# The second rows in front of a feed-forward: both engines evict every turned tile, in pairs

## The reference

```
x = layer_norm(ALPHA * x + 0.5 * swiglu(x, ffn1_w13[i], ffn1_w2[i]), ln_g[i, 0], ln_b[i, 0])
y = mixer(x) ; x = layer_norm(ALPHA * x + y, ln_g[i, 1], ln_b[i, 1])
x = layer_norm(ALPHA * x + 0.5 * swiglu(x, ffn2_w13[i], ffn2_w2[i]), ln_g[i, 2], ln_b[i, 2])

def swiglu(x, w13, w2):
    gate, up = jnp.split(x @ w13, 2, axis=-1)
    return (jax.nn.silu(gate) * up) @ w2
```

## Time and profile before

| | us |
|---|---|
| time, median of 3 runs | 2527.92 (2527.87 to 2528.9) |
| the profiled execution, its own time | 2527.56 |
| its span | 2525.8 |
| TensorE busy | 2463.6 (98%) |
| VectorE busy | 1505.4 (60%) |
| ScalarE busy | 1184.3 (47%) |
| GpSimd busy | 399.0 (16%) |

### The profile page before, as it was taken

The page is one execution under the profiler, slowest core; times in us unless marked ns, Lnnn a source line. Parts: engine busy times, 40 slices in busy tenths (PEclk is TensorE's granted clock), DMA queues, the critical chain, the costliest instruction groups (busy, mean ns, idle before and its releaser), DMA issues.

```text
span 2525.8 us, 32691 instructions
## 1 busy us (share of the span) xinstructions
PE 2463.6 (98%) x13213; PEld 2073.0 (82%) x13213; DVE 1505.4 (60%) x2146; ACT 1184.3 (47%) x1488; POOL 399.0 (16%) x463
## 2 busy tenths in 40 slices
PE   8999999999999999999989999999999999899999
PEld 6888878888888788888877888888878877898998
DVE  5546664464455645645566446446766567897644
ACT  5544554444444544444465444444554446444442
POOL 0002310000001100000131000001239802570000
PEclk9999999999999999999999999999999999999999
DMA  8554445555654455555334555555435543336553
GB/s 245 183 185 154 145 139 184 186 180 184 187 164 134 134 184 191 176 184 190 118 123 148 185 187 178 185 186 161 141 126 192 186 148 101 117 118 200 172 193 127
DMA packets 315542, 418.09 MB, mean 166 GB/s; under 512 B 18825, under 2 KB 273154, under 8 KB 315394
## 3 DMA queue, kind: packets, MB, share of 16 engines
q1 hardware_dynamic: 315394, 416.01, 51.2%
HBM read 414.92 MB, written 1.05 MB: 165 GB/s over the span
## 4 chain that ended last, share of the span: by engine, by line
PE 86%; DVE 6%; ACT 3%; issue 3%; POOL 1%; DMA 1%; SPq 0%; DVEq 0%; POOLq 0%; ACTq 0%
PE ps L597 25%; PE ps L599 24%; PE ps L598 24%; DVE wlo L469 2%; PE ps L614 2%; PE ps L2007 2%; PE ps L615 2%; PE ps L619 2%; PE ps L2264 1%; ACT whi L461 1%; PE ps L2313 1%; PE ps L2298 1%; PE ps L2253 1%; PE ps L1966 1%; DMA raw<-in_ffn_w_dram 1%
## 5 line engine op out<-in xcount | busy, mean ns | idle before, releaser
L469 DVE TENSOR_TENSOR wlo<-raw,whi 128x2048 fp32r<-128x2048 f32 (+1 forms) x397 | 909.5, 2296 | 608.3 <-ACT whi L461 607.5
L461 ACT ACTIVATE whi<-raw 128x2048 fp32r<-128x2048 f32 (+4 forms) x401 | 746.6, 1867 | 467.0 <-DMA raw<-in_ffn_w_dram 405.6
L597 PE MATMUL ps<-whi,xh 128*128 128x512 f32 (+3 forms) x1853 | 695.0, 375 | 8.5 <-DVE wlo L1386 2.5
L599 PE MATMUL ps<-whi,xl 128*128 128x512 f32 (+3 forms) x1853 | 687.7, 371 | 0.0
L598 PE MATMUL ps<-wlo,xh 128*128 128x512 f32 (+3 forms) x1853 | 687.3, 371 | 0.0
L597 PEld LDWEIGHTS ps<-whi,xh 128*128 128x128 f32 x1853 | 350.9, 189 | 73.7 <-issue 8.5
L599 PEld LDWEIGHTS ps<-whi,xl 128*128 128x128 f32 x1853 | 350.5, 189 | 60.0
L598 PEld LDWEIGHTS ps<-wlo,xh 128*128 128x128 f32 x1853 | 350.8, 189 | 57.8
L597 PE MATMUL ps<-whi,oh 128*128 128x512 f32 x944 | 380.0, 403 | 0.0
L599 PE MATMUL ps<-whi,ol 128*128 128x512 f32 x944 | 369.1, 391 | 0.0
L598 PE MATMUL ps<-wlo,oh 128*128 128x512 f32 x944 | 367.9, 390 | 0.0
(11 more groups left out here) (339 smaller groups left out, 2658.7 us busy)
## 6 DMA issues: line engine op xcount, KB each, us to landing
raw<-in_ffn_w_dram SPq DMA_DIRECT2D x352, 512.0 KB, 4.8
raw<-in_ffn_w_dram SPq DMA_DIRECT2D x88, 1024.0 KB, 4.9
raw<-in_w_ff_dram SPq DMA_DIRECT2D x32, 1024.0 KB, 5.3
raw<-in_w_out_dram SPq DMA_DIRECT2D x20, 1024.0 KB, 4.9
raw<-in_w_in_dram SPq DMA_DIRECT2D x20, 1024.0 KB, 5.1
raw<-in_dsa_w_in_dram SPq DMA_DIRECT2D x32, 512.0 KB, 4.8
raw<-in_dsa_w_in_dram SPq DMA_DIRECT2D x12, 1024.0 KB, 5.1
raw<-in_fox_w_in_dram SPq DMA_DIRECT2D x16, 512.0 KB, 4.6
```

The source lines that it names most:

```text
L461: act.activation(hi(u)[:, 0:w], raw[:, (slot[u] + 1) % SLOTS, 0:w], ACT.Copy).then_inc(sem("hi_ready"), 1)
L469: dve.tensor_tensor(lo(u)[:, 0:w], raw[:, (slot[u] + 1) % SLOTS, 0:w], hi(u)[:, 0:w].bitcast(F32), ALU.subtract).then_inc(sem("lo_ready"), 1)
L597: pe.matmul(o, ah, bh, start=start, stop=False, skip_group_check=True)
L599: return pe.matmul(o, al, bh, start=False, stop=stop, skip_group_check=True)
```

## The change

It concerns the second rows (t = 1) of the norms whose next stage is a feed-forward of the first block (`by_pairs`): seven of them. There `xT` is written by VectorE alone, all eight tiles, and `xh` by ScalarE alone, straight from PSUM with gain and shift in eight narrow activations instead of wide ones from `xT`. The turned tiles lie in banks 2, 3, 6 and 7 instead of 2, 5, 6 and 7. In each half ScalarE starts with the first two tiles and VectorE with the other two; then they change banks. The new semaphores `xh_half` and `xt_half` say that the first pair of each is done. VectorE takes the low part of a half directly behind that half's evictions. TensorE waits for both halves of `xn` before it turns the first one, begins the second rows' products with `xh_half`, and waits for the whole half (`middle`) in front of the third tile. GpSimd's `cx` waits for VectorE only.

```
+        if st["kind"] == "norm" and st["next"]["kind"] == "ffn":
+            made.update(xt_act=2, xh_half=2, xt_half=2)
...
-            first = 2 if t and st["next"]["kind"] == "ffn" else 4
-            bank = (first, 5, 6, 7)[k // 2]
+            bank = ((2, 3, 6, 7) if t and st["next"]["kind"] == "ffn" else (4, 5, 6, 7))[k // 2]
...
+        def by_pairs(st, t):
+            return t and st["kind"] == "norm" and st["next"]["kind"] == "ffn"
...
# token_major
                 for i, k in enumerate(ks):
+                    if i == 2 and middle:
+                        middle()
...
# GpSimd
-                            pool.wait_ge(sem("xt_act"), b("xt_act", 0) + 2 * t + h + 1)
+                            if not by_pairs(st, t):
+                                pool.wait_ge(sem("xt_act"), b("xt_act", 0) + 2 * t + h + 1)
...
# ScalarE, turned
+                        if by_pairs(st, t):
+                            for k in range(4 * h, 4 * h + 4):
+                                g = 8 * st["g"] + k
+                                if k == 4 * h + 2:
+                                    act.wait_ge(sem("xt_half"), b("xt_half", 0) + h + 1)
+                                last = act.activation(xh[:, k, tok], tb(st, t, k), ACT.Identity, bias=shifts[:, g:g + 1], scale=gains[:, g:g + 1])
+                                if k == 4 * h + 1:
+                                    last.then_inc(sem("xh_half"), 1)
+                            last.then_inc(sem("xh_ready"), 1)
+                            continue
...
# VectorE
+                def rest(t, h):
+                    tok = slice(t * P, (t + 1) * P)
+                    dve.wait_ge(sem("xh_ready"), b("xh_ready", 0) + 2 * t + h + 1)
+                    if by_pairs(st, t):
+                        dve.wait_ge(sem("xt_dve"), b("xt_dve", 0) + 2 * t + h + 1)
+                    dve.tensor_tensor(xl[:, 4 * h:4 * h + 4, tok], xT[:, 4 * h:4 * h + 4, tok],
+                                      xh[:, 4 * h:4 * h + 4, tok].bitcast(F32), ALU.subtract).then_inc(sem("xl_ready"), 1)
...
                     for h in range(2):
                         dve.wait_ge(sem("t_done"), b("t_done", 0) + 2 * t + h + 1)
+                        if by_pairs(st, t):
+                            for k in (4 * h + 2, 4 * h + 3):
+                                g = 8 * st["g"] + k
+                                last = dve.tensor_scalar(xT[:, k, tok], tb(st, t, k), gains[:, g:g + 1], shifts[:, g:g + 1], ALU.mult, ALU.add)
+                            last.then_inc(sem("xt_half"), 1)
+                            dve.wait_ge(sem("xh_half"), b("xh_half", 0) + h + 1)
                         for k in (4 * h, 4 * h + 1):
...
                         last.then_inc(sem("xt_dve"), 1)
+                        if by_pairs(st, t):
+                            rest(t, h)
...
# TensorE, turn_norm
+                        if by_pairs(st, t) and h == 0:
+                            pe.wait_ge(sem("xn_dve"), n("xn_dve", 0) + 2)
...
# TensorE, feed-forward
+                        middle = (lambda: high_ready(t, m)) if i == 0 and t and u else None
...
                     for m in range(2):
-                        high_ready(1, m)
+                        if u:
+                            pe.wait_ge(sem("xh_half"), b("xh_half") - 1 + m)
+                        else:
+                            high_ready(1, m)
                         used(up(0, m, 1))
```

More of the change, by code:

```diff
@@ L607, in feature_major, with token_major @@
             return last
-        def token_major(pe, o, u, c0, n, t, ks, width, k0=0, first=True, final=True, only=None, low=None):
+        def token_major(pe, o, u, c0, n, t, ks, width, k0=0, first=True, final=True, only=None, low=None, middle=None):
             if low:
                 for i, k in enumerate(ks):
+                    if i == 2 and middle:
+                        middle()
                     x, c = xh[:, k0 + k, t * P:(t + 1) * P], i * width + c0
@@ L1370, in turned @@
                         last.then_inc(sem("xt_dve"), 1)
-                    for h in range(2):
+                        if by_pairs(st, t):
+                            rest(t, h)
+                    for h in range(0 if by_pairs(st, t) else 2):
                         if h and between:
@@ L1375, in turned @@
                             ahead_of_last()
-                        dve.wait_ge(sem("xh_ready"), b("xh_ready", 0) + 2 * t + h + 1)
-                        dve.tensor_tensor(xl[:, 4 * h:4 * h + 4, tok], xT[:, 4 * h:4 * h + 4, tok],
-                                          xh[:, 4 * h:4 * h + 4, tok].bitcast(F32), ALU.subtract).then_inc(sem("xl_ready"), 1)
+                        rest(t, h)
                 if kind == "init":
@@ L1995, in up @@
                     def up(i, m, t, only=None):
+                        middle = (lambda: high_ready(t, m)) if i == 0 and t and u else None
                         low = (lambda: x_ready(t, m)) if i == 0 and only is None else None
                         return token_major(pe, ps[:, 4 + t, :], A(i) + m, 0, 512, t, range(4), 512,
-                                           k0=4 * m, first=m == 0, final=m == 1, only=only, low=low)
+                                           k0=4 * m, first=m == 0, final=m == 1, only=only, low=low, middle=middle)
                     def gturn(i):
```

## The result

The changed kernel takes **2537.26 us** (median of 5 runs, 2535.28 to 2538.86) against 2527.92 us of the kernel before in the same session (5 runs). The ratio is 1.0035, 95% interval 1.0023 to 1.0046: slower by 0.35%, 9.3 us. That lies above the range of the prediction (2526.3 to 2535.6). The profiled execution took 2537.79 us, with a span of 2536.0 us at a granted clock of 0.994 (before: 2525.8 us, 0.996).

A forecast was written before the change was run, and what follows sets the result against it. TensorE was taken to bound the kernel (86% of the chain of waits), a second chain through ScalarE and VectorE beside it. Terms 2.58 + 0.27 + 1.0 = +3.85 us gave 2531.6 us, range 2526.3 to 2535.6.

The forecast's parts named there:

- within 0.2%: Whole run: a time within 5.1 us of the kernel before, not told from no change; chance 0.66.
- The wait for `xh` and its 3.85 us: TensorE's wait before the second rows' first product, seven places: it goes; at most 7 x 0.55 = 3.85 us to win.
- ScalarE held at its seventh eviction, +0.86 us: ScalarE's last pair waits for VectorE's pair behind the subtraction, so the next weights' high part starts 0.86 us later.
- the first term of the sum: Three places behind a projection: the turn of the gated product goes later by 3 x 0.86 = +2.58 us.
- GpSimd's `cx` against the subtraction of half 0: nothing if it comes behind.: Both wait for the same VectorE pair: no cost if `cx` comes behind the subtraction, +0.55 us if ahead.
- rival 2: GpSimd's `cx` goes ahead of VectorE's subtraction and delays all behind it: +7.7 us, 2535.4 us; chance 0.15.
- The sign that I had named for being wrong: In the new trace, VectorE's subtraction of half 0 taking longer than 1 us would show the forecast wrong.
- Behind a feed-forward, 3 x 0.09: Three places behind a feed-forward: slack hides most of the delay, the turn's loads end 0.09 us later each, +0.27 us.
- The sines' place, +1.0 us: Place at 1879 us, with GpSimd's long sines work: +1.0 us, taken between 0.6 and 1.42 us.
- TensorE's first wait, +0.03: Transposes also wait for VectorE's half of `xn`: they and everything behind start 0.03 us later.
- The Trainium skill's rule that I had cited against small tiles: SBUF latency is paid per instruction, so tiles of 512 elements and more are preferred; spoke against the narrow tiles.

The follow-up runs named there:

- experiment 1: The changed kernel with VectorE's low part of half 0 moved between the two pairs of half 1: 2528.82 us, ratio 0.9998 to the kernel before.
- experiment 2: The changed kernel with GpSimd's `cx` of the second rows waiting for the low part of its half: 2534.26 us, ratio 1.0022 to the kernel before.
- experiment 10: The changed kernel timed again without any edit: 2535.83 us, ratio 1.0028 to the kernel before.
- experiment 3: The changed kernel with GpSimd's long sines work waiting until both gated products of the first slice are made: 2534.99 us, ratio 1.0024 to the kernel before.

## Why the prediction was wrong

The direction and the first mechanism were right; the amount was not, and the likeliest outcome ("within 0.2%") wasn't the one that came.

- *The wait for `xh` and its 3.85 us.* Right: it is gone in all seven places, and nothing comes of it, since a second chain ends later.
- *ScalarE held at its seventh eviction, +0.86 us.* Right as a cause (experiment 1 takes the whole loss away) and in its size (experiment 2: +0.94). What was mis-sized in the first term of the sum is what comes on top of it.
- **The step that failed: "GpSimd's `cx` against the subtraction of half 0: nothing if it comes behind."** I set VectorE ready 0.04 us behind its pair, and GpSimd 0.23 us. They start 0.10 and 0.08 us behind it. The 0.23 us were from a place where `cx` has a second wait in the program, for ScalarE's tiles, which the change takes away. That wait held nothing there, as this row of the kernel before shows: ScalarE's tiles were done at 1243.35 + 0.81 = 1244.16, before VectorE's (1244.38).

```profile
1243.35 0.81 ACT L881 ACTIVATE xT<-ps,shifts,gains 128x128 f32<-128x128 f32 x2 [1.10 <-PE ps L1966]
```

  Still 0.23 us passed with it and 0.08 pass without it; in experiment 2, where `cx` has a second wait again, for the subtraction, it starts 0.16 us behind that (355.95, 356.11). That the second wait itself costs time is the likely reading, and no run tests it by itself. For VectorE waiting on its own last result I had no row and took the gap of a crossing. The lead of 0.19 us that decided the order came from two rows of other situations, and a collision worth 0.45 us in seven places hung on it. It was rival 2, priced at +7.7 us and given 0.15; with such a margin it deserved about as much as the forecast. The three terms behind a projection came out at 3 x 1.40 for 3 x 0.86 (rival 2: 1.41). The sign that I had named for being wrong, a subtraction of half 0 longer than 1 us, is the one that came (1.14).
- *Behind a feed-forward, 3 x 0.09.* Wrong cover. I compared `gt` of the second rows with the turn (0.65 us to spare), and the low part with TensorE's arrival for the next slice. The next slice's first product waits for `gt` of the first rows too, which stands behind that low part and gives its bank back. VectorE at the place near 541 us, before:

```profile
550.78 0.42 DVE L1504 TENSOR_TENSOR gt<-sg,ps 128x256 f32<-128x256 f32 x1
```

  That ended at 551.20 and TensorE came at 551.73. With the 0.11 us from `gt` to the load (362.59 to 362.70) there were 0.42 us to spare, and 1.39 - 0.42 = 0.97 is what was measured there (0.97 to 1.03 in the three); even the forecast's own 0.86 would have cost 0.44, five times the 0.09. The same `gt` is behind the 1.45 us at L602, which the weight loads' row puts down to `wlo`: `wlo` was done at 362.25, and the product's own row has `gt` (17.3 us of idle time ahead of L602 on the page, most of it by L1537):

```profile
L602 PE MATMUL ps<-whi,xh 128*128 128x512 f32 (+3 forms) x1853 | 695.1, 375 | 17.3 <-DVE gt L1537 10.7
```

- *The sines' place, +1.0 us.* Right in size (+0.83, +0.80), and the subtraction does get in ahead. Not foreseen: TensorE's idle time there grew from 0.70 to 2.05 us, and the clock fell behind it in one of two traces of the change, which cost 1.6 us (2.41 - 0.83).
- *TensorE's first wait, +0.03.* 0.05 a place.
- *The chances.* 0.66 for "within 0.2%" is less than its own parts: five sixths of 0.62, and 0.10 and 0.06, make 0.68 before anything unseen.

How much each step weighs: the places of the first trace sum to +9.6 us where the forecast has +3.85, 5.8 more. The collision has 6 x 0.45 = 2.7 of them behind projections and feed-forwards, the crossings 6 x 0.08 = 0.5, the wrong cover about 1.2, the clock 1.6; the sines' place without the clock came 0.2 us under its term. The collision is the largest, and without its 2.7 us the measured +9.3 would be +6.6, inside the range. The clock's fall was chance: experiment 10, whose trace hasn't got it, measured +7.4 us, just inside the range's upper end of +7.7, which rival 2 had set.

The Trainium skill's rule that I had cited against small tiles ("VectorE: DVE Perf Modes", the TRN2 errata) did not decide: experiment 1 has the same small tiles and none of the loss. (The two rows that I had set beside it aren't alike either: the 128-column evictions read PSUM, the 512-column subtraction reads SBUF.) The other one that I had cited from the Trainium skill, on SBUF interfaces shared by GpSimd and VectorE ("GPSIMD Engine Reference", "Specifications"), did. The traces agree with it: the subtraction, with two inputs in SBUF, takes 1.14 us beside `cx`, while in experiment 1 VectorE's evictions from PSUM that run beside this `cx` (355.04 to 355.76) keep their 0.72 us:

```profile
355.21 0.63 POOL L757 TENSOR_SCALAR cx<-xT 128x512 f32<-128x512 f32 x1 [3.46 <-DVE xT L1403]
```

What stays open: which of the two engines wins such a race if the margin is small. In the two traces of the change GpSimd started 0.01 or 0.02 us ahead in each of the fourteen places, so it is steady here, but no run shifted one of the two by a few hundredths of a microsecond to see the order turn.

## What to carry to other kernels

Where a change lets one event release two engines that disturb each other, take the race as lost until a row shows the same two waits, and give neither order a small chance on a lead, here 0.19 us, that comes from rows of other situations. In an engine's in-order queue, first comes what another engine stands waiting for: moving one subtraction behind the next pair of tiles gave the whole loss back. And before a shift is called covered, look at every wait that stands on its way, not at the last one: here the buffer that `gt` gives back was needed sooner than its result.

## What the runs showed of the hardware

- A 128x512 VectorE subtraction with both inputs in SBUF took 0.69 us alone, 1.14 us behind a GpSimd instruction of 0.62 us that had started 0.02 us earlier, and 2.42 us behind one of 1.90 us. In both of these it ended 0.54 us behind the end of the GpSimd instruction. So it lost nothing where it started late enough: in experiment 1 the subtraction of half 0 started 0.16 us before the end of `cx` (355.68, 355.84) and took its 0.69 us. It works both ways: a GpSimd instruction that took 1.90 us took 2.33 when the subtraction was ahead of it.
- VectorE waiting for its own last instruction started 0.10 us behind its end (355.40, 355.50), GpSimd waiting for the same instruction 0.08 us behind it. ScalarE's high part, for which the subtraction waits too, isn't the reason: in half 1 of experiment 1 it was done at 356.61, the pair at 357.02, and the subtraction started at 357.12, again 0.10 us behind the pair.
- The granted clock at a place where TensorE stands still and goes on: it fell to 0.50 behind 2.05 us (first trace of the change) and 2.19 us (experiment 2), and stayed at 1.00 behind 2.04 (experiment 10), 1.41 (experiment 1), 1.24 (experiment 3) and 0.70 us (before). So about the same idle time went both ways in two executions of one kernel. The Trainium skill, "TensorE: Matmul & The Clock Gate", section "Part 1: The HAM clock gate", says of the clock's rise at a kernel's start that it comes at another point from run to run of one kernel; these two traces show such a difference for a fall in the middle of one.
